# Tables loaded in two parts, the memory tile behind the value tiles, and row sums and head norms in another order

## What is computed

```
h = rmsnorm(x, g) @ w_in_e          # split into qa ka va qb kb vb
qa, ka, qb, kb = rmsnorm over each head's 64 columns
A (8 heads, 2 key heads): s = qa.ka/8 - slope_h*|i-j|, masked beyond 128
   m = max(max_j s, sink_h);  p = exp(s-m) / (sum exp(s-m) + exp(sink_h-m))
B (8 heads): s = qb.kb/8 + bias table;  p = softmax(s)
x = x + concat(p_A @ va, p_B @ vb) @ w_out_e
xk, xv = rmsnorm(mem, g_mem) @ w_mem_kv      # used by the third layer
```

## Time and profile before

| what | value |
|---|---|
| median of 3 runs | 1023.01 us (1022.87 to 1023.74) |
| the profiled execution, its own time | 1024.58 us |
| its span, first to last instruction | 1022.8 us |
| mean granted TensorE clock | 0.999 of full speed |
| PE busy | 1002.8 us, 98% of the span |
| PE weight loads busy | 892.1 us, 87% |
| DVE, ACT, POOL busy | 648.6, 488.3, 137.8 us |
| moved from memory | 172.79 MB read, 1.05 MB written |

### The profile page before, as it was taken

The page is one execution under the profiler, slowest core; times in us unless marked ns, Lnnn a source line. Parts: engine busy times, 40 slices in busy tenths (PEclk is TensorE's granted clock), DMA queues, the critical chain, the costliest instruction groups (busy, mean ns, idle before and its releaser), DMA issues.

```text
span 1022.8 us, 15392 instructions
## 1 busy us (share of the span) xinstructions
PE 1002.8 (98%) x6194; PEld 892.1 (87%) x6194; DVE 648.6 (63%) x916; ACT 488.3 (48%) x746; POOL 137.8 (13%) x173
## 2 busy tenths in 40 slices
PE   8889999999999999999999999999999999999997
PEld 7668879999998998888889999999887889999995
DVE  4687756664555655666666554455767887657674
ACT  5575536444554533234545444454545445545452
POOL 0631004970000200110001000000550110000000
PEclk9999999999999999999999999999999999999999
DMA  9963345465456544335464456545544463354541
GB/s 343 295 206 124 103 145 165 171 207 199 165 190 211 176 166 165 124 124 206 165 206 163 167 178 215 183 166 172 197 168 141 133 190 124 124 165 125 173 157 42
DMA packets 106933, 174.82 MB, mean 171 GB/s; under 512 B 4080, under 2 KB 66672, under 8 KB 106864
## 3 DMA queue, kind: packets, MB, share of 16 engines
q1 hardware_dynamic: 106144, 173.01, 50.9%
q10 hardware_dynamic: 720, 0.83, 0.2%
HBM read 172.79 MB, written 1.05 MB: 170 GB/s over the span
## 4 chain that ended last, share of the span: by engine, by line
PE 91%; DMA 3%; DVE 3%; SPq 1%; issue 1%; POOL 1%; ACT 1%; DVEq 0%; POOLq 0%
PE ps L456 23%; PE ps L382 20%; PE ps L384 19%; PE ps L383 19%; PE ps L582 2%; DMA raw<-in_memT 2%; PE ps L553 1%; PE ps L508 1%; PE ps L728 1%; PE ps L565 1%; DMA raw<-in_w_in_e 1%; PE ps L716 1%; DVE wlo L1297 0%; DVE arena L1396 0%; PE ps L535 0%
## 5 line engine op out<-in xcount | busy, mean ns | idle before, releaser
L1297 DVE TENSOR_TENSOR wlo<-raw,whi 128x1024 fp32r<-128x1024 f32 x314 | 373.8, 1229 | 30.3 <-ACT whi L904 13.9
L904 ACT ACTIVATE whi<-raw 128x1024 fp32r<-128x1024 f32 x314 | 317.4, 1049 | 95.5 <-PE ps L384 50.5
L382 PE MATMUL ps<-hTh,whi 128*128 128x256 f32 (+1 forms) x872 | 249.1, 286 | 0.4
L384 PE MATMUL ps<-hTh,wlo 128*128 128x256 f32 (+1 forms) x872 | 246.8, 283 | 0.0
L383 PE MATMUL ps<-hTl,whi 128*128 128x256 f32 (+1 forms) x872 | 246.8, 283 | 0.0
L382 PEld LDWEIGHTS ps<-hTh,whi 128*128 128x128 f32 (+1 forms) x872 | 166.8, 191 | 3.9 <-issue 1.9
L383 PEld LDWEIGHTS ps<-hTl,whi 128*128 128x128 f32 (+1 forms) x872 | 166.8, 191 | 1.2
L384 PEld LDWEIGHTS ps<-hTh,wlo 128*128 128x128 f32 (+1 forms) x872 | 166.8, 191 | 0.0
L382 PE MATMUL ps<-whi,hTh 128*128 128x512 f32 (+1 forms) x376 | 150.7, 401 | 6.3 <-DVE wlo L1297 2.3
L384 PE MATMUL ps<-whi,hTl 128*128 128x512 f32 (+1 forms) x376 | 145.3, 386 | 0.0
L383 PE MATMUL ps<-wlo,hTh 128*128 128x512 f32 (+1 forms) x376 | 145.1, 386 | 0.0
(11 more groups left out here) (185 smaller groups left out, 1131.7 us busy)
## 6 DMA issues: line engine op xcount, KB each, us to landing
raw<-in_w SPq DMA_DIRECT2D x64, 1024.0 KB, 5.4
raw<-in_w_in SPq DMA_DIRECT2D x34, 1024.0 KB, 5.2
raw<-in_w_in_o SPq DMA_DIRECT2D x24, 1024.0 KB, 5.4
raw<-in_w_out_o SPq DMA_DIRECT2D x8, 1024.0 KB, 5.0
raw<-in_w_in_e SPq DMA_DIRECT2D x7, 1024.0 KB, 14.5
raw<-in_w_mem SPq DMA_DIRECT2D x4, 1024.0 KB, 7.0
raw<-in_w_out_e SPq DMA_DIRECT2D x4, 1024.0 KB, 4.9
raw<-in_w_out SPq DMA_DIRECT2D x4, 1024.0 KB, 5.2
```

The costliest lines, as they stand in the source:

```text
L382: e.matmul(o, a[0], b[0], start=start, stop=False)
L384: return e.matmul(o, a[1], b[0], start=False, stop=stop)
L904: e.activation(split_half(i)[0], raw_half(i), ACT.Copy).then_inc(*up("hi", ("hi", i)))
L1297: e.tensor_tensor(l, raw_half(i), h.bitcast(F32), ALU.subtract).then_inc(*up("lo", ("lo", i)))
```

## The change

- Tile order: vb comes before memT, so the halves are now kb 10 to 13, vb 14 to 17, memT 18 and 19, xk 20 to 23.
- SP: after tile 4 come 393 KB of constants and 24 columns of the row vector (semaphore `c`); after tile 14 the other 524 KB of constants and 1024 columns of the row vector (semaphore `c2`, for which POOL's decays wait). The constants for the sinks' scales are gone.
- Scores of A: they are now held in units of the dot product (distance times 8 over the slope's inverse is added), so the exponential's scale is 0.125 for all heads, and one operation on DVE (L1405 of the changed kernel) takes the place of two (L1402, L1404).
- Row sums of x: on ACT ahead of the first half of qb's high parts, on DVE likewise.
- The memory's row sums: one block in step 4 and one in step 5 on ACT, ahead of the step's exponential; on DVE in steps 6 and 7.
- Step 3 on PE: the half of vb ahead of the transposes of qb; step 6: the half of vb ahead of the transposes of kb. On ACT in step 3 the halves and kb's squares come ahead of storing qb.
- DVE: the step's low parts come ahead of hn_scaled, hn_sums, v_stored and the row reciprocals.
- The broadcast of the memory's row scales moves from step 7 to 9, and the scaling of xk on DVE from steps 9 and 11 to 10 and 12.
- PE: transposes of B's output for oe tiles 2 and 3 come in step 18 ahead of the last half of oe tile 1, before after it.

```diff
@@ weight_tiles
     rows_first("kb", "w_in_e", 1280, 512)
+    rows_first("vb", "w_in_e", 1792, 512)
     rows_first("memT", "memT", 0, 256)
-    rows_first("vb", "w_in_e", 1792, 512)
@@ sp_program
-                if m == 3:
-                    e.dma_start(cst[:, 128:NCONST], A["consts"][:, 128:NCONST]).then_inc(S["c"], 16)
-                    e.dma_start(rows[:, :], bass.AP(A["rowvec"].tensor, 0, [[0, 128], [1, NROW]])).then_inc(S["c"], 16)
+                if m == 4:
+                    e.dma_start(cst[:, 128:C_COS], A["consts"][:, 128:C_COS]).then_inc(S["c"], 16)
+                    e.dma_start(rows[:, R_SINK:NROW], bass.AP(A["rowvec"].tensor, R_SINK, [[0, 128], [1, NROW - R_SINK]])).then_inc(S["c"], 16)
+                if m == 14:
+                    e.dma_start(cst[:, C_COS:NCONST], A["consts"][:, C_COS:NCONST]).then_inc(S["c2"], 16)
+                    e.dma_start(rows[:, 0:R_SINK], bass.AP(A["rowvec"].tensor, 0, [[0, 128], [1, R_SINK]])).then_inc(S["c2"], 16)
@@ pe_program
+                if 3 <= s < 7:
+                    n_half("vb", s - 3, 512, "E")
                 if s == 3:
                     hn_transposed("qb")
+                    value["wd", first_half["memT"]] = value["wd", first_half["memT"] + 1] = value["wd", first_half["vb"]]
                 if s == 6:
                     hn_transposed("kb")
-                if 3 <= s < 7:
-                    n_half("vb", s - 3, 512, "E")
-                if s == 7:
+                if s == 9:
                     broadcast("mem")
...
+                    if s == 18:
+                        for k in range(2, 4):
+                            transposes(("oe", k), osb, 2 * k, [("o", "B", 0), ("o", "B", 1)])
                     w.wait_ge(*at("xl", "oe", i))
                     acc_half("E", ("oe", i), x, hT, 2 * i, start=s == 15)
-            for i in range(2, 4):
-                transposes(("oe", i), osb, 2 * i, [("o", "B", 0), ("o", "B", 1)])
@@ act_program
+                if key == "AB" and s in (4, 5):
+                    row_squares("mem", osb, osb, [(S["m"], 16), (S["m"], 16)], (s - 4,))
...
-            used("qa", 2)
+            weights_to(6)
             row_squares("E", x3, osb, [(S["x0"], 16), (S["x1"], 16)])
...
+                if 3 <= s < 7:
+                    used("vb", s - 3)
                 if s == 3:
+                    hn_squares("kb")
                     hn_stored("qb")
-                    hn_squares("kb")
-                if s == 4:
-                    row_squares("mem", osb, osb, [(S["m"], 16), (S["m"], 16)])
@@ dve_program
-                        d = e.scalar_tensor_tensor(Sb[:, j, :], b[:, j, :], 0.125 * 2.0 ** (h + 1), negabs[:, qb, :], ALU.mult, ALU.add)
+                        d = e.scalar_tensor_tensor(Sb[:, j, :], negabs[:, qb, :], 8 * 2.0 ** -(h + 1), b[:, j, :], ALU.mult, ALU.add)
...
-                    e.tensor_tensor(mx, mx, skp[:, hsl], ALU.max).then_inc(*up("dst", ("mxs", key, i)))
-                    w.wait_ge(*at("mxs", key, i))
-                    e.tensor_tensor(nm, mx, negs[:, hsl], ALU.mult).then_inc(*up("dst", ("nm", key, i)))
+                    e.scalar_tensor_tensor(nm, mx, -0.125, nsk[:, hsl], ALU.mult, ALU.min).then_inc(*up("dst", ("nm", key, i)))
...
+            weights_to(6)
+            row_reciprocals("E")
             used("qa", 3)
-            row_reciprocals("E")
             hn_sums("qa")
...
+                if s < 3:
+                    used("kb", s + 1)
+                if 3 <= s < 7:
+                    used("vb", s - 3)
+                if 7 <= s < 11:
+                    used(("xk", (s - 7) // 2), (s - 7) % 2)
                 if s == 1:
                     hn_scaled("qb")
...
-                    row_reciprocals("mem")
+                if s in (6, 7):
+                    row_reciprocals("mem", (s - 6,))
                 if s == 7:
                     v_stored("vb", bvv[:, 0, :], "E")
```

More of the change, by code:

```diff
@@ L24 @@
 NROW = 1048
-C_ID, C_NA, C_CA, C_COS, C_SIN, C_U, C_L, C_IS, C_NS = (
-    0, 128, 640, 896, 1024, 1152, 1536, 1920, 1928)
-NCONST = 1936
+C_ID, C_NA, C_CA, C_COS, C_SIN, C_U, C_L = 0, 128, 640, 896, 1024, 1152, 1536
+NCONST = 1920
 NRAW, NHI, NLO = 4, 6, 5
@@ L34 @@
 SEMS = ["mm", "wd", "tp", "qk", "pv", "hi", "xh", "aev", "ex", "asq", "lo", "xl", "dev", "dst", "sc", "po",
-        "w0", "w1", "w2", "w3", "w4", "raw0", "raw1", "raw2", "raw3", "x0", "x1", "t0", "t1", "t2", "t3", "t4", "id", "c", "g", "b", "m", "out"]
+        "w0", "w1", "w2", "w3", "w4", "raw0", "raw1", "raw2", "raw3", "x0", "x1", "t0", "t1", "t2", "t3", "t4", "id", "c", "c2", "g", "b", "m", "out"]
 PAIRS = [(0, 2), (1, 3), (4, 6), (5, 7)]
@@ L227, in program @@
         negabs = v3(cst, 2, C_NA, 512)
-        invs, negs = cst[:, C_IS:C_IS + 8], cst[:, C_NS:C_NS + 8]
-        skp, hb = lgt[:, 0:8], lgt[:, 8:32]
+        nsk, hb = lgt[:, 0:8], lgt[:, 8:32]
         xT0 = av(XT, 2048, 8)
@@ L645, in pe_program @@
                     n_half("kb", 0, 512, "E")
-                    value["wd", first_half["memT"]] = value["wd", first_half["memT"] + 1] = value["wd", first_half["kb"]]
                 att_step("AB", s)
@@ L908, in used, with row_squares @@
                 weights_to(first_half[label] + j + HI_AHEAD)
-            def row_squares(stage, src, junk, needs):
-                for tb in range(2):
+            def row_squares(stage, src, junk, needs, blocks=range(2)):
+                for tb in blocks:
                     w.wait_ge(*needs[tb])
@@ L985, in att_exp @@
                     if key == "A":
-                        scl, nm = 2.0 ** -(h + 1), stats(("nm", "A", qb), 8)[:, h:h + 1]
+                        scl, nm = 0.125, stats(("nm", "A", qb), 8)[:, h:h + 1]
                     else:
@@ L1064, in act_program @@
                     used("kb", s + 1)
+                if 3 <= s < 7:
+                    used("vb", s - 3)
                 if s == 3:
+                    hn_squares("kb")
                     hn_stored("qb")
-                    hn_squares("kb")
-                if s == 4:
-                    row_squares("mem", osb, osb, [(S["m"], 16), (S["m"], 16)])
                 if s == 6:
                     hn_stored("kb")
-                if 3 <= s < 7:
-                    used("vb", s - 3)
                 if s == 7:
                     v_stored("vb", 0, 512, bvv[:, 1, :], "E")
+                if s == 9:
                     stored_broadcast("mem")
@@ L1301, in used, with row_reciprocals @@
                 weights_to(first_half[label] + j + LO_AHEAD)
-            def row_reciprocals(stage):
-                for tb in range(2):
+            def row_reciprocals(stage, blocks=range(2)):
+                for tb in blocks:
                     i = stats(("i", stage, tb), 1)
@@ L1575, in dve_program @@
                 att_step("AB", s)
+                if s < 3:
[4 more added lines that the diff above has]
+                    used(("xk", (s - 7) // 2), (s - 7) % 2)
                 if s == 1:
                     hn_scaled("qb")
-                if s < 3:
-                    used("kb", s + 1)
                 if s == 3:
@@ L1583, in dve_program @@
                     hn_scaled("kb")
-                    row_reciprocals("mem")
-                if 3 <= s < 7:
-                    used("vb", s - 3)
+                if s in (6, 7):
+                    row_reciprocals("mem", (s - 6,))
                 if s == 7:
                     v_stored("vb", bvv[:, 0, :], "E")
-                if 7 <= s < 11:
-                    used(("xk", (s - 7) // 2), (s - 7) % 2)
-                if s in (9, 11):
-                    c = (s - 9) // 2
+                if s in (10, 12):
+                    c = (s - 10) // 2
                     w.wait_ge(*at("mm", ("xk", c), 0))
@@ L1929, in pool_program @@
             w.wait_ge(S["c"], 32)
-            e.tensor_tensor(skp, rows[:, R_SINK:R_SINK + 8], invs, ALU.mult).then_inc(*up("po", ("skp",)))
+            e.tensor_scalar(nsk, rows[:, R_SINK:R_SINK + 8], -1.0, None, ALU.mult).then_inc(*up("po", ("nsk",)))
             hn_scales("qb")
```

7 lines of the change are left out of this document (2 added, 5 removed).

## The result

The changed kernel takes 1021.69 us (median of 22 runs, 1019.77 to 1022.73), the kernel before 1023.02 in the same sessions (22 runs). The ratio is 0.9983, with a 95% interval of 0.9976 to 0.9990: about 1.3 us faster, inside the 0.2% that was taken as no change, and 4.7 us above the forecast of 1017.0. Its profiled execution took 1021.98, so its rows stand for the median; before's had taken 1024.58.

A forecast was written before the change was run, and what follows sets the result against it. PE was taken to bound the kernel, its stops from 25 to 151 us costing 10.5 us with restarts. With 4.5 left, the gain of 6.0 took the median from 1023.01 to 1017.0, range 1015.2 to 1020.9.

The forecast's parts named there:

- Steps 1 to 6: Row sums, tables, memory tile, orders on PE and DVE, output tile: PE's loss falls from 10.5 to 4.5 us.
- the prediction's own signs of being wrong: In the profile after: ACT waiting for memT, over 3 us before B0's scores, or a new stop after the mixer.
- Rival (b): POOL's power keeps its 2.60 us because DVE's low part starts first: 1.0 less gain, 1018.0; chance 0.13.
- the time 1017.2: By an exclusive DVE-POOL lock, the low part of qb's second half waits some 1.6 us and PE loses 0.2.
- rival (d): Slower: memT's first half lands late for ACT, each us after 56.3 costs one; 1025.7 at 65; chance 0.05.
- The stop before A4: PE waits for A4's scores until ACT has read qb's transposes: a new stop of 0.8 us.
- All five terms: Left losses: qb's second tile 0.2, A4's scores 0.8, B0's scores 2.0, B1's transposes 0.5, output tile 1.0; together 4.5.
- (a): Waits change places: additional high and low parts before B0's bank, 0.8 more at A4; 1020.0, chance 0.24.
- (c): No change: stops return one for one at the banks, or the steps do not take hold; 1022.5, chance 0.10.
- both bank stops: Waits before A4's and B0's scores, 0.8 and 2.0 us; bounds from 0 up to 1.2 and 3.7.
- the least gain of 3.9: Lower bound of the gain, with the stops before A4's and B0's scores as long as 1.2 and 3.7 us.

The follow-up runs named there:

- e12: The e1 kernel with 28 additional matmuls on PE ahead of B0's scores, where PE stood still: 1019.71 us.
- e5: The changed kernel with 18 additional matmuls on PE before A4's scores and 18 before B0's: 1019.32 us.
- e3: The e1 kernel, with DVE also reading vb's value tile before its low parts in the kernel's step 7: 1017.06 us.
- e9: The e7 kernel with only the row sums of x put back behind qb's first half: 1017.79 us.
- e10: The e7 kernel with both tables (constants, row vector) loaded whole behind tile 3: 1016.97 us.
- e11: The e7 kernel with the memory tile memT back ahead of vb: 1015.72 us.
- e7: The e3 kernel, plus memory reciprocal and xk's scaling ahead of DVE's low parts, and B's last output transposed between two token blocks: 1014.34 us.
- e8: The changed kernel with only the row sums of x put back behind qb's first half: 1021.74 us.
- e2: The changed kernel with 16 additional matmuls on PE ahead of A4's scores: 1020.67 us.
- e1: The changed kernel with ACT storing qb's transposes ahead of memT's first half and kb's squares: 1021.47 us.

## Why the prediction was wrong, step by step

**Which stops go and come: right.** Steps 1 to 6 named them, and they are as named. None of the prediction's own signs of being wrong appeared either (ACT waiting for memT, more than 3 us before B0's scores, a new stop after the mixer). qa's sums on DVE are at 23.59, and its second block at 29.41, 5.8 behind them, where 5.7 was worked out. The power is short in both halves. Timelines of POOL and of DVE of the changed kernel, as in the earlier trace rows:

```profile
24.73 1.67 POOL L1881 TENSOR_TENSOR stat<-stat 128x8 f32<-128x8 f32 x1
```

```profile
24.79 1.22 DVE L1300 TENSOR_TENSOR wlo<-raw,whi 128x1024 fp32r<-128x1024 f32 x1
```

The power began 0.06 ahead of the low part and took 1.67; the low part took 1.22 and was not held, as at 45 us before. Rival (b) falls with these two rows, and so does the time 1017.2 by the Trainium skill's rule of an exclusive lock. vb's tile landed for ACT at 44.2 (44 foretold), and ACT never waited for memT: rival (d) falls.

**The stop before A4: mis-sized, 0.8 with its restart became 1.9.** Timeline of ACT of the changed kernel:

```profile
56.39 1.69 ACT L901 ACTIVATE urh<-raw,gain 128x256 fp32r<-128x256 f32 x4
57.99 1.05 ACT L924 ACTIVATE arena<-ps 128x512 f32<-128x512 f32 x2
58.94 1.25 ACT L931 ACTIVATE arena<-ps,gain 128x512 f32<-128x512 f32 x2
```

ACT's chain is the one foretold, memT's first half, kb's squares, qb's storing; the first bank is read at 59.6, as worked out. PE was there at 59.67 - 1.74 = 57.9 and not at 58.9, since its first inputs had landed 1.1 earlier. The rows of before came from an execution 1.57 above the median, and its late inputs were part of that. I corrected the sum for it and not the places: whoever arrives earlier waits longer at the next bank. All five terms together were 4.5 and came out at 5.9, which is 1.4 of the 4.7 us by which the forecast was missed, and 1.1 of it is this stop.

**The failed step: the price of a stop.** The sum went by idle time plus 0.16 for each stop, and the places to look at by "full granted clock". That is what the profile of before showed, with stops of 1.70 and 1.65 and no fall behind them. It is not the price of a long stop. In the changed kernel the stop of 1.74 cost about 1.74 + 0.16 + 3.4 = 5.3. The forecast gave 4.5 as lost; the lost time was 5.9 + 3.4 = 9.3. The 3.4 is half of 6.8 us at half clock; by what e12 measured (1.5 for 3.4) it is 3.0, and by the medians of e5 it is 2.4. Without the fall the time would have been near e5's 1019.3: inside the range, but still 2.3 above the forecast. No rival had it: (a), the waits changing places, would have asked for more high and low parts in the queues, which are not there. The small difference of (c) came about by another way than (c) said.

**Slips of the sum.** With both bank stops at nothing the left time is 4.5 - 2.8 = 1.7 and the gain 8.8, not 7.8, so the range should have begun at 1014.2. Rival (a)'s gain of 3.0 lies below the least gain of 3.9 that the bounds allow. In (d) a landing at 57 costs 0.7 and not 0.9. None of them bears on the miss.

**What the change is worth** therefore depends on the two banks behind it. With them free and the clock whole, e3 is 5.9 us below the kernel before, for the change and the two moves together, and e9, e10 and e11 price its parts at 3.4, 2.6 and 1.4 in e7, the first two with a fall of the clock in some of the runs.

**Open.** The same length of stop, 1.7 to 2.0 us, was followed by a fall in some executions and not in others (1.70: none in before, falls in e8 and e9; 2.02: none in the changed kernel, 2.03: a fall in e2). In the profiles the longer ones, 2.46, 2.63 and 3.75, all were, and none of 1.36 or less was. Why the first fall in the changed kernel lasts 6.8 us and all others 3.4 was not tried. Nor is it shown why the kernel before hardly gets slower when its mean clock is lower, nor where the last 0.9 us is: e5 stands 2.3 above the forecast, and the stops are 1.4 of that.

## What to carry to other kernels

When PE bounds a kernel, time made for it early is worth only what the next held bank lets through: follow the earlier PE to each bank and buffer in turn, and free these first, by moving the operation that reads the bank ahead of the work queued on its engine. Price a stop of PE with the granted clock behind it, which neither the busy time nor the list of waits shows; in this kernel stops of 1.7 us and more could cost 1.5 to about 3 us beyond their length, and the kernels whose stops were 1.36 at most never paid it. Measure the price between two rows of the same work with and without the fall, and not from medians, whose runs mix both. And where the profiled execution stands above the median, find out what in it was late before adding up places from it.

## What the runs showed of the chip that was not expected

- TensorE's clock fell to half after stops of 1.7 to 3.75 us in the middle of a stretch that was otherwise full, for 3.4 us at a time, once 6.8. By the windows it began between the restart itself (e1: 82.0, restart 82.09) and 1.6 us behind it (e8: 35.2, restart 33.58).
- Useless matmuls in the idle time keep the clock up: the medians fall by 1.8 us in e12 and 2.4 in e5, and the rows of e12 show 1.5 gained for 3.4 at half clock.
- A power on POOL that began 0.06 us ahead of a subtraction on DVE held it up in no way, twice (45 us before, 24.7 us after), while one that began 0.14 behind it took 2.60 instead of 1.65. A scaling on POOL that began 0.01 us ahead of two such subtractions (31.53 and 31.54 in the changed kernel) took 2.42 us, the next of its shape 0.27; the subtractions took their usual 2.35 together. Where an operation of such a pair took longer than usual, it was the one on POOL.
